# SBUF start addresses of a hybrid decoder layer: the inputs of the long products are moved by 64 bytes, to the same offset modulo 256 as the weights

## The reference

```python
x = x + 0.5 * swiglu(rms_norm(x, norm_ffn1), ffn1_gate, ffn1_up, ffn1_down)     # 1024 -> 2816 -> 1024
h = rms_norm(x, norm_mix)
qa, ka, va, rb, kb, vb, ga, gb = split(h @ w_in)                                 # 1024 -> 5120
y_a = moba_attention(qa, ka, va, rel_bias)                                       # 8 heads of 64, one block of 256
y_b = rwkv7_time_mix(h, rb, kb, vb, ...)                                         # 8 heads of 64, low-rank (LoRA) gates
x = x + (sigmoid(ga) * (y_a @ proj_a) + sigmoid(gb) * (y_b @ proj_b)) @ w_out
x = x + 0.5 * swiglu(rms_norm(x, norm_ffn2), ffn2_gate, ffn2_up, ffn2_down)
return rms_norm(x, norm_final)
```

## The kernel before

| tiles | before | after |
|---|---|---|
| `w_raw`, `w_hi`, `w_lo`, `lora_whi`, `lora_wlo`, `x`, `cst` (its first two 128x128 matrices) | 128 | 128 |
| `hhi_f`, `hlo_f`, `hid_hi_t`, `hid_lo_t`, `silu`, `prod`, `out_tok`, `x_tok` | 64 | 128 |
| `hhi_m`, `hlo_m`, `yahi`, `yalo`, `ybhi`, `yblo`, `mhi`, `mlo`, `mg`, `pa` | 64 | 128 |
| `bct`, `kct` | 64 | 128 |
| `vt`, `AX`, `NA`, `RR`, `KK`, `G`, `state`, `X1`, `qk`, `va`, `pt`, `lg` | 192 | 0 |
| `kkn`, `tmp`, `aa`, `AR`, `kt`, `gg`, `gates` | 64 | 64 |
| `r`, `k`, `v`, `dec` | 128 | 128 |

## Time and profile before

### The profile page before, as it was taken

How to read it: one execution, slowest core, us unless ns; L and a number is a source line. 1 busy time by engine, 2 the same in 40 slices (tenths; PEclk the granted TensorE clock), 3 DMA queues, 4 the chain that set the end, 5 groups by cost and what they waited for, 6 DMA issues and landing times.

```text
span 622.4 us, 15455 instructions
## 1 busy us (share of the span) xinstructions
PE 612.2 (98%) x6716; PEld 597.0 (96%) x6716; DVE 421.0 (68%) x493; ACT 296.9 (48%) x345; POOL 89.4 (14%) x90
## 2 busy tenths in 40 slices
PE   9999999999999999999999999999999999999996
PEld 8899999999999999999988889999999999999996
DVE  5757787765556369968994336977767666665663
ACT  6734555444434274434665544644644444443332
POOL 0116900000114000020005524004000000000130
PEclk9999999999999999999999999999999999999999
DMA  8677656656555345585232222365566656556551
GB/s 287 217 229 236 201 183 186 191 169 200 177 189 200 98 136 190 190 187 159 91 120 87 71 86 77 103 201 183 179 196 202 202 185 187 186 170 208 181 166 67
DMA packets 100672, 105.40 MB, mean 169 GB/s; under 512 B 2244, under 2 KB 98732, under 8 KB 100628
## 3 DMA queue, kind: packets, MB, share of 16 engines
q1 hardware_dynamic: 99380, 101.47, 50.9%
q0 software_dynamic: 1088, 3.02, 2.2%
q10 hardware_dynamic: 160, 0.27, 0.1%
HBM read 103.50 MB, written 1.25 MB: 168 GB/s over the span
## 4 chain that ended last, share of the span: by engine, by line
PE 83%; DVE 8%; ACT 4%; DMA 3%; issue 1%; SPq 0%; ACTq 0%; DVEq 0%
PE two L1467 24%; PE two L1468 23%; PE two L1469 23%; PE two L1463 10%; DVE w_lo L905 4%; ACT w_hi L532 2%; DMA w_raw<-in_ffn_up 1%; DMA w_raw<-in_ffn_down 1%; DMA w_raw<-in_ffn_gate 1%; DMA x_tok<-in_x 1%; PE two L1741 1%; PE two L1742 1%; PE two L1743 1%; DVE gates L1110 0%; PE two L1886 0%
## 5 line engine op out<-in xcount | busy, mean ns | idle before, releaser
L532 ACT ACTIVATE w_hi<-w_raw 128x2048 fp32r<-128x2048 f32 (+1 forms) x86 | 162.5, 1890 | 244.4 <-PE two L1469 214.8
L905 DVE TENSOR_TENSOR w_lo<-w_raw,w_hi 128x2048 fp32r<-128x2048 f32 (+1 forms) x86 | 199.5, 2320 | 84.0 <-ACT w_hi L532 83.7
L1467 PE MATMUL two<-hlo_f,w_hi 128*128 128x256 f32 x640 | 177.8, 278 | 1.7 <-DVE w_lo L905 1.7
L1468 PE MATMUL two<-hhi_f,w_lo 128*128 128x256 f32 x640 | 177.4, 277 | 0.0
L1469 PE MATMUL two<-hhi_f,w_hi 128*128 128x256 f32 x640 | 177.4, 277 | 0.0
L1467 PEld LDWEIGHTS two<-hlo_f,w_hi 128*128 128x128 f32 x640 | 120.8, 189 | 2.7 <-DVE w_lo L905 2.2
L1468 PEld LDWEIGHTS two<-hhi_f,w_lo 128*128 128x128 f32 x640 | 120.9, 189 | 0.0
L1469 PEld LDWEIGHTS two<-hhi_f,w_hi 128*128 128x128 f32 x640 | 120.9, 189 | 0.0
L1467 PE MATMUL two<-hid_lo_t,w_hi 128*128 128x256 f32 x352 | 97.7, 278 | 0.7
L1468 PE MATMUL two<-hid_hi_t,w_lo 128*128 128x256 f32 x352 | 97.2, 276 | 0.0
L1469 PE MATMUL two<-hid_hi_t,w_hi 128*128 128x256 f32 x352 | 97.2, 276 | 0.0
(11 more groups left out here) (344 smaller groups left out, 981.9 us busy)
## 6 DMA issues: line engine op xcount, KB each, us to landing
w_raw<-in_ffn_up SPq DMA_DIRECT2D x21, 1024.0 KB, 5.4
w_raw<-in_ffn_gate SPq DMA_DIRECT2D x20, 1024.0 KB, 5.4
w_raw<-in_w_in SPq DMA_DIRECT2D x20, 1024.0 KB, 5.0
w_raw<-in_ffn_down SPq DMA_DIRECT2D x16, 896.0 KB, 4.6
w_raw<-in_ffn_down SPq DMA_DIRECT2D x8, 1024.0 KB, 5.0
w_raw<-in_w_out SPq DMA_DIRECT2D x4, 1024.0 KB, 5.0
w_raw<-in_proj_a SPq DMA_DIRECT2D x4, 512.0 KB, 3.7
w_raw<-in_proj_b SPq DMA_DIRECT2D x4, 512.0 KB, 4.3
```

The source lines that it names most:

```text
L532: nc.scalar.activation(whi[slot][:, 0:kts], raw[slot][:, 0:kts], ACT.Copy).then_inc(sg["hi_ready"], 1)
L905: nc.vector.tensor_tensor(wlo[slot][:, 0:kts], raw[slot][:, 0:kts], whi[slot][:, 0:kts].bitcast(F32), ALU.subtract).then_inc(sg["lo_ready" ...
L1467: mm(dst, whi[slot][:, k_, cols], xl, start=start, stop=False)
L1468: mm(dst, wlo[slot][:, k_, cols], xh, start=False, stop=False)
```

## The change

Three lines of tile declarations. A pad of 192 bytes ahead of the inputs of the feed-forward blocks goes, so that all tiles behind it in that scope start 192 bytes lower. A pad of 64 bytes is put ahead of the inputs of the mixing block, so that all tiles behind it start 64 bytes higher; the pad ahead of the low-rank weights shrinks by the same 64 bytes, so these stay. `pad_y` (128 bytes, line 290) stays as it is, and what follows it moves by 64 bytes. The list of instructions, their operands' shapes and their waits are the same on all five engines.

```diff
@@ the scope of the feed-forward blocks @@
             h_f = sb("h_f", [P, KD, T], scope=sc)
-            sb("pad_f", [P, 48], scope=sc)
             hhi_f = sb("hhi_f", [P, KD, T], F32R, scope=sc)
@@ the scope of the mixing block @@
             gates = mb("gates", [P, 2 * KD, T])
+            mb("pad_m", [P, 16])
             yahi = mb("yahi", [P, HT, T], F32R)
@@ the low-rank weights @@
-                mb("pad_lora", [P, 48], scope=sc)
+                mb("pad_lora", [P, 32], scope=sc)
                 lora_whi = mb("lora_whi", [P, KD, 5 * P], F32R, scope=sc)
```

## The result

The changed kernel takes 645.81 us (median of six runs, 644.31 to 646.82). Its time over that of before is 1.0333, with a 95% interval of 1.0294 to 1.0372: slower by 3.3%. The six runs of before taken with it lie between 622.69 and 632.67 us with a median of 629.88; the ratio goes by the faster runs of before and leaves out those near 632 us, so it is not 645.81 over 629.88. The span of the profiled execution is 645.0 us, against 622.4.

What follows compares the result with a forecast made beforehand. The prediction took TensorE's long products times their pace as the bound: 17.0 us for slower products, less 1 us hidden in the recurrence, on 622.4 plus 0.4 us, gives 638.8 us; range 618 to 650 us.

Steps and rivals of the forecast that it cites:

- What bounds the kernel: TensorE, busy 612.2 of 622.4 us: the time is the number of matmuls times their pace plus little.
- That the offset between the two reads acts: All 4,632 long products: the offset between moving and stationary operand goes from 64 to 0, which slows them.
- Small matmuls and other engines at nothing: Recurrence matmuls stay at 1.16 us for 64; VectorE under 1 us either way; other engines' accesses cost nothing.
- The price of a product: Long products: each pays the slow pace's 4.43 ns above the fast one; 3,832 steps give 17.0 us.
- the 672 that are slow already add nothing: Long products already at the slow pace of 117.77 ns keep it, adding no time.
- worse than seen: Rival, long products: another step of the same size, 122.2 ns a product, 36.9 us more, 659.7 us; chance 0.10.
- The window 40:80: Sign in the new trace: some 342 matmuls if right, 355 no effect, 359 or more faster, under 335 worse.
- Two readings of before: Long products before: 128 steps are breaks; slow ones stand in some 19 stretches, the first at 201.5 us.
- What hides it: Feed-forward blocks: nothing, the 4.2 us of `w_lo` waits being no slack; recurrence: 1 us off, leaving +16.0 us.
- No effect: Rival, long products: the offset may not matter, so the sum is zero and the time 622.8 us; chance 0.25.
- Faster: Rival, all long products: the disturbance goes and each runs at 112 ns, -9 us, 613.8 us; chance 0.12.
- Partly slow: Rival, long products: pace picked at each restart, half of the fast steps turn slow, +8.5 us, 631 us; chance 0.09.

Runs made afterwards that it cites:

- experiments 2 to 4 and 13: Feed-forward part of the change alone 640.37 us, mixing part alone 632.32; changed kernel with all tiles 64 bytes later 645.14; kernel before with all tiles 64 bytes later 622.76.
- same_again: The kernel before, unedited, run and profiled once more: 624.58 us against 623.83, ratio 1.0013.
- best_shifted: The kernel before with a 64-byte pad ahead of every tile (weights at 192, inputs at 128, difference still 192): 622.76 us, ratio 0.9979.
- all_shifted: The changed kernel with a 64-byte pad ahead of every tile (weights and inputs at 192, difference still 0): 645.14 us, ratio 1.0335.
- sweep_a: The kernel before with pads resized: difference 64 in gate and up products, 128 in down products, 64 in the mixing block: 636.31 us, one run.
- fine_c: The kernel before with gate and up products at difference 192 by an offset inside the tiles, and down products at 196: 631.10 us.
- mix_only: The kernel before with only the mixing block's part of the change: 632.32 us, ratio 1.0160.

## Why the prediction was right or wrong

**What bounds the kernel**: right. TensorE's list is the time, and the growth is all in the long products. **That the offset between the two reads acts**, stage by stage, on all of them, and through the difference: right, shown by experiments 2 to 4 and 13. The prediction wrote the difference without its sign, as 64, and so had the value products at the same place as the others. **Small matmuls and other engines at nothing**: right, 1.16 us for 64 as before, VectorE within 0.7 us.

**The price of a product**: the step that failed. The prediction took the slow pace of before, 117.77 ns, as what difference 0 would cost, "each product pays what the disturbed stretches pay now". The slow pace turned out to be the second pace of difference 192, and the only one of 64. Difference 0 has its own, 119.93 ns. So the term of 4.43 ns for 3,832 steps, 17.0 us, should have been 6.59 ns, 25.3 us; and "the 672 that are slow already add nothing" should have been 1.5 us. The growth of the price was right in kind and 2.2 ns a product too small. Two paces of one place had been read as "undisturbed" and "disturbed", when they said nothing on how bad another place can be. The case *worse than seen* (122.2 ns) was nearer in kind, since it let the price go beyond both known paces, but it took a step of 4.4 ns where 2.2 was right. The window 40:80 had 336 matmuls, between the 342 that the prediction gave as the sign of being right and the "under 335" of *worse than seen*.

**Two readings of before** were off, by little. Of the 128 breaks, 17 are products at the lower clock, as shown above. And the slow stretches don't begin at 201.5 us: three short ones, 29 steps, lie at 9 to 21 us.

**What hides it**: wrong too, in the other direction. The waits for `w_lo` were taken for restarts behind TensorE's own last product, which slower products don't fill, and 1 us was taken off for the recurrence. This is the waits view after:

```profile
PEld two L1601 <- DMA x_tok<-in_x: 2.3, 2, 2.0
PEld two L1463 <- issue: 2.1, 9, 0.3
```

Its two longest rows are shown; the wait for `w_lo`, 4.2 us before, is not among the rows of 0.3 us or more, and the chain lies on VectorE for 1% where it had 8%. That isn't chance: the three profiles at difference 192 in block 1 and in the mixing block (before, `same_again`, `best_shifted`) have 4.2, 3.5 and 3.7 us of it, the two at difference 0 throughout (after, `all_shifted`) none in their waits view. The breaks gave back 3.9 us, mostly in the feed-forward blocks, of which 1.7 us is the stretch at the lower clock and not the change. The rest TensorE used up: rounding and remainder of a chunk have to keep up with 48 products, and these now give them 5.76 us in place of 5.44. The two errors partly cancel, which is luck: 16.0, and 9.8 for the price, less 2.9 for what the breaks gave back beyond the 1 us allowed, is 22.9; +22.6 was measured for the span. Against the ratio of the runs, 3.3%, the forecast of 2.6% was short by a quarter, and set against the six runs of before taken with the result it was short by more than half, because their median lay 7 us above that of the first three.

**The rivals.** *No effect* and the Trainium skill's rule that went with it ("SBUF — State Buffer", "Who interferes with whom": two independent ports) fall, at 113.3 against 120.0 ns. The Trainium skill's page "TensorE: Matmul & The Clock Gate", section "Step-by-step: what each phase is for", says that loading the next tile's weights takes no read bandwidth from the running matmul. Here the trace doesn't agree: with the same loads and streams a product takes 113.3 or 120.0 ns, by the addresses of the two alone. *Faster* falls: its argument against itself, that streams of unlike speed pass each other at some residue wherever they start, fits that nearly all differences are slow. What it doesn't explain is why 192 alone escapes, in so narrow a place. *Partly slow* falls: only nine steps of the changed kernel are at the fast pace. The 109.2 ns for 256 columns, by the Trainium skill's page "TensorE: Matmul & The Clock Gate", section "Wait — 56ns, not 53.3ns?", is an estimate that no run came to; no stage of any profile averages less than 113.3 ns where all streams are full.

**What stays open.** How SBUF serves the two reads, why the curve has the steps that it has, and what picks the slow pace at 192 after a break. Only 0 and 192 were run at a second place of the weights, so for the other differences, the fine ones above all, a part of the absolute offset is not excluded. No kernel was found that beats before. What is left there is the slow steps, 672 x 4.4 ns = 3 us in the first profile; 91 of them are the value products at 64, which in `sweep_a`, at 192, were at the fast pace in half of their steps.

## What to carry to other kernels

In this kernel, where TensorE works through full weight loads and full streams of float32r side by side, its pace depends on the difference of the two operands' start addresses modulo 256, sign included. In a kernel like it, read the pace as matmuls per window, and sweep it with pads in steps of 32 bytes, with all tiles of a group of products alike. A pad ahead of one tile shifts all behind it, so a harmless-looking allocation can move the pace of a whole stage; if a kernel bound by TensorE changes by some per cent with the same instruction list, compare addresses first. If a trace shows two paces for one operation, the slower one is no bound for a third setting. And look up the granted clock over every stretch that is counted as waiting: 17 full products had passed for breaks.

## What the runs showed of the hardware that was not expected

- One pair of operands at one pair of addresses has two stable paces, 113.3 and 117.8 ns at difference 192. It changes between them at breaks, but for one case in 65 in three profiles, and keeps the fast one for 1,263 products (block 2 of before), the slow one for 959 (`fine_c`).
- The fast place at 192 ends within 4 bytes above (196: 120.5 ns) and within 8 below (184: 120.0; 188 was not run), and repeats after 256 bytes (448).
- At difference 0 the step is 120 ns almost without exception, at 200 it goes 119, 125, 116 by line in nearly every triple.
- With two of three streams halved, a triple takes 340 ns at difference 0 and 341 at 192: the cost of the offset shows only where the streams are full.
- Just after an idle time of 1.49 us in the first profile of before, TensorE's granted clock was 0.50 for 3.4 us, and a long product took 213 ns in place of 113. Behind an idle time of 1.15 us at the same place, `mix_only` kept a clock of 1.00; it is one case of each.
